# Moving half of the attention steps beside the values' product, in a fused two-block transformer kernel

## What is computed

```python
def even_mixer(h, w_in, w_out):                 # the first layer, "e" in the kernel
    qkv = (h @ w_in).reshape(B, S, 3, 16, 64).transpose(2, 0, 3, 1, 4)
    q, k, v = rope(qkv[0]), rope(qkv[1]), qkv[2]
    a = moba_attention(q[:, :8], k[:, :8], v[:, :8])     # here: plain causal softmax attention
    b = dilated_mixture(q[:, 8:], k[:, 8:], v[:, 8:])    # three windows, mixed by their sums
    return concatenate([a, b]) @ w_out

def diff_attention(q, k, v, lam):               # the second layer, "d"
    s = einsum('bhcqd,bhckd->bhcqk', q, k) * scale       # 8 heads, two maps each (c = 0, 1)
    p = softmax(where(kpos <= qpos, s, -inf))
    a = p[:, :, 0] - lam * p[:, :, 1]
    return einsum('bhqk,bhkd->bhqd', a, v)               # v has 128 columns per head
# then rms_norm per head, times a gain, and @ w_out
```

## Time and profile before

| what | value |
|---|---|
| median of three runs | 3159.81 us (3157.5 to 3160.11) |
| the profiled execution | 3160.78 us, its span 3159.0 us |
| TensorE busy | 3105.3 us, 98% of the span |
| weight loads into TensorE | 2495.2 us, 79% |
| VectorE busy | 1584.0 us, 50% |
| ScalarE busy | 1118.4 us, 35% |
| GpSimd busy | 20.4 us, 1% |
| mean granted TensorE clock | 0.994 of 2.4 GHz |
| attention "e", from the values' product on | 110.28 to 236.96 us of the span |
| attention "d", from the values' product on | 730.45 to 864.02 us |

### The profile page before, as it was taken

How to read it: one execution, slowest core, us unless ns; L and a number is a source line. 1 busy time by engine, 2 the same in 40 slices (tenths; PEclk the granted TensorE clock), 3 DMA queues, 4 the chain that set the end, 5 groups by cost and what they waited for, 6 DMA issues and landing times.

```text
span 3159.0 us, 35038 instructions
## 1 busy us (share of the span) xinstructions
PE 3105.3 (98%) x13927; PEld 2495.2 (79%) x13932; DVE 1584.0 (50%) x2346; ACT 1118.4 (35%) x1730; POOL 20.4 (1%) x29
## 2 busy tenths in 40 slices
PE   8989999999999999999999999999999999999998
PEld 6748888887588888877788878888777888878887
DVE  5575675355566752554523463334654424453324
ACT  3254443223644432334323243322334323333322
POOL 1000000000000000000000000000000000000000
PEclk9999999999999999999999999999999999999999
DMA  5302222243022223412223223333412223223321
GB/s 189 114 8 87 100 94 97 97 140 100 1 94 94 96 98 100 139 43 93 66 95 94 94 83 102 96 94 107 121 49 78 80 94 94 88 92 99 95 94 67
DMA packets 86337, 289.30 MB, mean 92 GB/s; under 512 B 11304, under 2 KB 11320, under 8 KB 85920
## 3 DMA queue, kind: packets, MB, share of 16 engines
q1 hardware_dynamic: 83584, 278.96, 27.6%
q0 software_dynamic: 1440, 6.00, 0.5%
q10 hardware_dynamic: 1152, 2.10, 0.2%
HBM read 272.33 MB, written 2.10 MB: 87 GB/s over the span
## 4 chain that ended last, share of the span: by engine, by line
PE 94%; DVE 3%; ACT 2%; issue 1%; DMA 0%; POOL 0%; ACTq 0%; DVEq 0%; POOLq 0%
PE banks L393 74%; PE banks L455 8%; PE banks L422 3%; PE banks L729 2%; PE banks L364 1%; PE banks L533 1%; PE banks L708 1%; PE banks L502 1%; PE banks L557 1%; PE banks L545 1%; PE banks L756 0%; PE banks L782 0%; ACT prob_e L875 0%; DMA x_resid<-x_fm 0%; DVE prob_e L1396 0%
## 5 line engine op out<-in xcount | busy, mean ns | idle before, releaser
L1252 DVE TENSOR_TENSOR w_lo<-w_raw,w_hi 128x1024 fp32r<-128x1024 f32 (+1 forms) x512 | 612.4, 1207 | 915.9 <-ACT w_hi L822 914.8
L822 ACT ACTIVATE w_hi<-w_raw 128x1024 fp32r<-128x1024 f32 (+1 forms) x512 | 526.8, 1041 | 843.2 <-PE banks L393 767.3
L393 PE MATMUL banks<-h_hi,w_hi 128*128 128x512 f32 x2304 | 713.8, 391 | 10.7 <-DVE h_lo L1339 10.7
L393 PE MATMUL banks<-h_lo,w_hi 128*128 128x512 f32 x2304 | 710.7, 390 | 0.0
L393 PE MATMUL banks<-h_hi,w_lo 128*128 128x512 f32 x2304 | 710.3, 390 | 0.0
L393 PEld LDWEIGHTS banks<-h_hi,w_hi 128*128 128x128 f32 x2304 | 431.9, 188 | 100.7 <-issue 12.3
L393 PEld LDWEIGHTS banks<-h_lo,w_hi 128*128 128x128 f32 x2304 | 433.5, 188 | 90.5
L393 PEld LDWEIGHTS banks<-h_hi,w_lo 128*128 128x128 f32 x2304 | 433.4, 188 | 90.1
L393 PE MATMUL banks<-hid_hi,w_hi 128*128 128x512 f32 x668 | 206.4, 390 | 0.0
L393 PE MATMUL banks<-hid_lo,w_hi 128*128 128x512 f32 x668 | 205.8, 389 | 0.0
L393 PE MATMUL banks<-hid_hi,w_lo 128*128 128x512 f32 x668 | 205.6, 389 | 0.0
(11 more groups left out here) (278 smaller groups left out, 3170.9 us busy)
## 6 DMA issues: line engine op xcount, KB each, us to landing
w_raw<-weights SPq DMA_DIRECT2D x496, 512.0 KB, 3.6
scratch<-scratch SPq DMA_DIRECT2D x128, 64.0 KB, 2.0
w_raw<-weights SPq DMA_DIRECT2D x16, 256.0 KB, 2.6
scratch<-scratch SPq DMA_DIRECT2D x32, 128.0 KB, 2.3
x_resid<-x_fm ACTq DMA_DIRECT2D x8, 256.0 KB, 10.5
decay<-tables POOLq DMA_DIRECT2D x2, 1024.0 KB, 6.1
y_fm<-x_resid SPq DMA_DIRECT2D x8, 256.0 KB, 2.1
rope<-tables POOLq DMA_DIRECT2D x2, 512.0 KB, 4.2
```

What stands on the lines that cost most here:

```text
L393: mm = e.matmul(bank[b][:, :], wt[:, k, j * P:(j + 1) * P], a[:, kt, :], start=kt == 0 and step == 0, stop=kt == k_tiles - 1 and step == 2)
L822: e.activation(m.w_hi[u % HL][:, 0:n], m.raw[u % RAW][:, 0:n], ACT.Copy).then_inc(*mark("w_hi", u))
L1252: e.tensor_tensor(m.w_lo[u % HL][:, 0:n], m.raw[u % RAW][:, 0:n], f32(m.w_hi[u % HL][:, 0:n]), ALU.subtract).then_inc(*mark("w_lo", u))
```

## The change

Both attentions take their first 24 of 48 steps (n = -1 to 4) during the values' product, as `UNDER_VALUES` says: one call in the first unit, which only starts the generator, then four, four, three, four, three, three, three. A step follows a group of six matmuls, and where a unit has four, the fourth follows the unit. `attention_steps` starts at n = -1, so the first two pairs' scores are steps of the same list. Within a step, the loop over c now stands around values and transposes. `exp` is an entry of its own, behind the transposes' copies on ScalarE.

`AttentionBanks` deals out the banks on all engines. Beside the product there are four, 4 to 7: in "e" scores and transposes take 4, 5 and 6 in turn, in "d" scores take 4 and 5, the transposes and head squares 6; the values take 7. Behind the product the banks are dealt much as before, with the scores beginning at 2 and 3. The six buffers of probabilities lie together (two of them had lain over `h_hi`), and the transposed probabilities have two buffers, where "e" had four. The value matmul of pair g waits only for the panel of v that holds it. VectorE's list changes in the same way as ScalarE's. Removed bodies that stand in the listing above are left out here.

```diff
-            prob_at = [big + kb * K for kb in (48, 53, 58, 63)] + [h, h + 5 * K]
+            prob_at = [big + kb * K for kb in (48, 53, 58, 63, 78, 83)]
             self.prob[st] = [at(f"prob{i}_{st}", [P, TRI_N], F32, a) for i, a in enumerate(prob_at)]
-            self.prob_t[st] = [at(f"probt{i}_{st}", [P, TRI_N], F32, big + (68 + 5 * i) * K) for i in range(4 if st == "e" else 2)]
+            self.prob_t[st] = [at(f"probt{i}_{st}", [P, TRI_N], F32, big + (68 + 5 * i) * K) for i in range(2)]
             self.rope[st] = at(f"rope_{st}", [P, 2 * S], F32, big + 80 * K)
...
-    def tm(self, beside):
+    def tm(self, beside, calls=None):
         for panel in range(2):
             for n in range(DT // 2):
                 self.next_unit()
+                for _ in range(calls[4 * panel + n] if calls else 0):
+                    next(beside, None)
                 if n == DT // 2 - 1:
                     yield panel
-                next(beside, None)
+                if not calls:
+                    next(beside, None)
         for _ in beside:
             pass
+UNDER_VALUES, LAST_UNDER = (1, 4, 4, 3, 4, 3, 3, 3), 4
+class AttentionBanks:
+    def __init__(self, st):
+        self.st, self.beside_product, self.pool, self.pairs, self.turns = st, True, 0, 0, 0
+    def from_pool(self):
+        self.pool += 1
+        return 4 + self.pool % 3
+    def scores(self):
+        if not self.beside_product:
+            self.pairs += 1
+            return 2 * (self.pairs % 2), 2 * (self.pairs % 2) + 1
+        return (self.from_pool(), self.from_pool()) if self.st == "e" else (4, 5)
+    def turn(self):
+        if not self.beside_product:
+            self.turns += 1
+            return 4 + self.turns % 2
+        return self.from_pool() if self.st == "e" else 6
+    def values(self, g):
+        return 7 if g <= LAST_UNDER - 2 else 6 + (g + 1) % 2
+def under_values(steps, do):
+    yield
+    for what, g, i, c in steps:
+        if what != "step_done":
+            do(what, g, i, c)
+            continue
+        yield
+        if (g, i) == (LAST_UNDER, 0):
+            return
 def attention_steps(st):
-    yield "inverse", 0, None
-    for kb in reversed(range(TB)):
-        yield "normalise", 0, kb
-    for n in range(1, DT + 3):
+    for n in range(-1, DT + 3):
         for kb in reversed(range(TB)):
             if n + 1 < DT:
...
+                yield "scores", n + 1, kb, None
+            for c in range(2 if st == "e" else 1):
+                if 2 <= n < DT + 2:
+                    yield "values", n - 2, kb, c
+                if 1 <= n <= DT:
+                    yield "transpose", n - 1, kb, c
+            if n + 1 < DT:
+                yield "exp", n + 1, kb, None
+            if 0 <= n < DT:
                 if kb == TB - 1:
-                    yield "inverse", n, None
-                yield "normalise", n, kb
+                    yield "inverse", n, None, None
+                yield "normalise", n, kb, None
             if st == "d" and n >= 3 and kb == 2:
-                yield "head_squares", n - 3, None
+                yield "head_squares", n - 3, None, None
             if kb:
-                yield "finish_some", None, None
+                yield "finish_some", None, None, None
+            yield "step_done", n, kb, None
         if st == "d" and n in HEAD_BATCHES:
-            yield "finish_next", *HEAD_BATCHES[n]
+            yield "finish_next", *HEAD_BATCHES[n], None
     if st == "d":
-        yield "finish_some", None, None
-        yield "finish_some", None, None
+        yield "finish_some", None, None, None
+        yield "finish_some", None, None, None
...
-    def gemm_tm(st, hi, lo, ready, evacuated, beside):
+    def gemm_tm(st, hi, lo, ready, evacuated, beside, calls=None):
...
+                steps = calls[4 * panel + kt0 // 2] if calls else 1
...
+                        if steps > 1 and (k, pair[0]) != (1, 2):
+                            next(beside, None)
                 if kt != DT - 1:
                     mm.then_inc(*mark("gemm", ("unit", u)))
-                next(beside, None)
+                if steps in (1, 4):
+                    next(beside, None)
         for _ in beside:
...
-        turn = {"s": 0, "t": 0}
-
-        def scores(g, i, score_banks=(0, 1, 2, 3)):
-            b = [score_banks[2 * (turn["s"] % 2) + c] for c in range(2)]
-            turn["s"] += 1
+        banks = AttentionBanks(st)
+        def scores(g, i):
+            b = banks.scores()
             width = (i + 1) * P
             w.wait_ge(*after("masks", 0))
             for c in range(2):
...
                          start=st == "e", stop=True, skip_group_check=True).then_inc(*mark("scores", (st, g, i, c)))
                 freed[b[c]] = ("exp" if st == "d" else "neg_max", (st, 2 * g + c, i))
...
+        def transpose(g, kb, c):
+            b, slot = banks.turn(), (2 * g + c) % len(prob)
             bank_is_free(b)
...
+            for i in range(kb, TB):
+                w.wait_ge(*after("normed", (st, 2 * g + c, i)))
+                t = e.transpose(bank[b][:, (i - kb) * P:(i - kb + 1) * P],
+                                prob[slot][:, TRQ[i] + kb * P:TRQ[i] + (kb + 1) * P], m.ident[:, :])
+            t.then_inc(*mark("transposed", (st, g, c, kb)))
+            freed[b] = ("probt_act" if (kb + c) % 2 == 0 else "probt_dve", (st, g, c, kb))
+        def values(g, kb, c):
+            b, width = banks.values(g), P // results
+            bank_is_free(b)
+            w.wait_ge(*after("v_act", (st, g // 4, 3)))
+            w.wait_ge(*after("v_dve", (st, g // 4, 2)))
+            w.wait_ge(*after("probt_act" if (kb + c) % 2 == 0 else "probt_dve", (st, g, c, kb)))
+            o = e.matmul(bank[b][c * width:(c + 1) * width, kb * P:S], v[:, kb, g * P + c * width:g * P + (c + 1) * width],
+                         prob_t[(g * results + c) % len(prob_t)][:, TRI[kb]:TRI[kb] + (TB - kb) * P],
+                         start=kb == TB - 1, stop=kb == 0, skip_group_check=True)
             if kb == 0:
-                freed[b] = ("o_copy", g) if st == "d" else ("o_lo", (st, g))
+                o.then_inc(*mark("values", (st, g, c)))
+                if c == results - 1:
+                    freed[b] = ("o_copy", g) if st == "d" else ("o_lo", (st, g))
...
-        gemm_tm(st + "v", m.h_hi, m.h_lo, ready, lambda panel, t: ("v_act" if t % 2 else "v_dve", (st, panel, t)), early_scores())
+        steps = attention_steps(st)
+        gemm_tm(st + "v", m.h_hi, m.h_lo, ready, lambda panel, t: ("v_act" if t % 2 else "v_dve", (st, panel, t)),
+                under_values(steps, do), UNDER_VALUES)
+        banks.beside_product = False
+        for what, g, i, c in steps:
+            do(what, g, i, c)
...
-        def scores(g, i):
+        def exp(g, i):
             width = (i + 1) * P
             for c in range(2):
-                n, b = 2 * g + c, score_banks[2 * (turn["s"] % 2) + c]
+                n = 2 * g + c
                 p = prob[n % len(prob)][:, TRQ[i]:TRQ[i] + width]
                 w.wait_ge(*after("neg_max", (st, n, i)))
                 if st == "e":
...
                                  accum_out=m.col(n, 1, i)).then_inc(*mark("exp", (st, n, i)))
                     continue
                 if g == 2:
-                    w.wait_ge(*after("gemm", ("tm", st + "v", 1, 3)))
+                    w.wait_ge(*after("roped", (st + "k", DT - 1)))
                 if g >= 3 and c == 0:
                     w.wait_ge(*after("transposed", (st, g - 3, c, 0)))
                 if g >= 3 and c == 1:
                     w.wait_ge(*after("normed", (st, 2 * (g - 3), 0)))
-                e.activation(p, bank[b][:, 0:width], ACT.Exp, bias=m.col(n, 0, i),
+                e.activation(p, bank[scored[c]][:, 0:width], ACT.Exp, bias=m.col(n, 0, i),
                              accum_out=m.col(n, 1, i)).then_inc(*mark("exp", (st, n, i)))
...
+        def transpose(g, kb, c):
+            b = banks.turn()
+            if (kb + c) % 2 == 0:
+                w.wait_ge(*after("transposed", (st, g, c, kb)))
+                width = (TB - kb) * P
+                e.activation(prob_t[(g * results + c) % len(prob_t)][:, TRI[kb]:TRI[kb] + width], bank[b][:, 0:width],
+                             ACT.Copy).then_inc(*mark("probt_act", (st, g, c, kb)))
+            b = banks.values(g)
...
+            if what == "scores":
+                scored = banks.scores()
+            elif what == "exp":
+                exp(g, i)
...
-                n, b = 2 * g, score_banks[2 * (turn["s"] % 2)]
-                turn["s"] += 1
+                n, (b, _) = 2 * g, banks.scores()
```

More of the change, by code:

```diff
@@ L924, in finish_heads, with do @@
             yield
[L926 to L933 removed]
+        finishing, scored, banks = iter(()), None, AttentionBanks(st)
+        def do(what, g, i, c):
+            nonlocal finishing, scored
+            if what == "scores":
+                scored = banks.scores()
+            elif what == "exp":
```

(18 more changed lines are left out.)

202 lines of the change are left out of this document (59 added, 143 removed).

## The result

| | us | against before |
|---|---|---|
| before, median | 3159.96 (3157.5 to 3160.47) | |
| after, median of 4 | 3196.47 (3195.66 to 3198.28) | ratio 1.0117, 95% interval 1.0104 to 1.0129 |
| after, span of the profiled execution | 3193.9 | before 3159.0 |

The change makes the kernel 36.5 us slower. The forecast was +24 us (3184). Its range, 3161 to 3200, holds the time. The sign and the two main causes were right, and 12 us were missing.

What follows compares the result with a forecast made beforehand. TensorE carries 94% of the chain and was taken to bound the kernel. Terms of +15.5 us in e and +8.4 in d summed to +23.9, giving 3184 us, with a range of 3161 to 3200.

Steps and rivals of the forecast that it cites:

- Is there anything to fill: e's stretches up to n=5: 80.7 us of TensorE work against 92.6 used, so better overlap can return 12 us there.
- Part 1, interruptions: Each entry of a step into the product costs TensorE 0.23 us: 5.5 us in e, 2.9 us in d.
- Part 2, the parted halves: e's value halves, with a transpose between, no longer run side by side: 3.38 us per head pair, seven times, 23.7 us.
- the upper bound for a lone half: In e, one value half alone costs 1.01 us at 512 columns, the price of the pair.
- Rival B: e's parted halves cost less, a lone half at d's price without form changes: 10.6 us, 3171 us; chance 0.17.
- Part 3, e's waits: e's waits for banks at the second panel's start (0.65 us) and the exit (1.1): 1.8 us together; masking is hidden.
- Part 4, d's single pair: Under d's product, scores on banks 4 and 5 wait for the previous step's exponentials: 18.6 us, bounds zero and 28.
- Clock 1.00 over both products: Expected sign in the trace: TensorE's mean clock at 1.00 over the values' products of both e and d.
- d behind the product: Exponentials behind the transposes' copies end TensorE's short waits there: -3 of 44.62 us, bounds 0 and -5.
- A: The forecast itself: e's parted halves and d's single banks cost what they show, 3184 us, range 3172 to 3198; chance 0.57.
- D: d's waits pull the clock down: ten more microseconds of matmuls at half speed, waits half longer, 3199 us; chance 0.12.
- C: The covered fill wins, with halves, transposes and banks at no price: -10 us each in e and d, 3140; chance 0.11.

Runs made afterwards that it cites:

- e6: The changed kernel with only eight score steps under the product in both attentions, e's value halves together, exponentials behind the copies: 3148.8 us, ratio 0.9964.
- e1: The changed kernel with e's two value halves of a step issued together again, then both transposes: 3174.8 us, ratio 1.0045.
- e3: The kernel before with the parting alone: e's value halves each followed by a transpose, all behind the product: 3179.0 us, ratio 1.0060.
- e2: The changed kernel with only d's first eight score steps under the product, on two pairs of banks, e unchanged: 3178.8 us, ratio 1.0059.
- e4: The changed kernel with 14 of d's steps under the product, two per unit, single score pair kept, e unchanged: 3183.2 us, ratio 1.0073.
- e5: The changed kernel with e's value halves together (24 steps), d's eight steps under the product, exponentials ahead of the copies in both: 3159.7 us, ratio 0.9997.
- e11: e6 with ScalarE's exponentials ahead of the transposes' copies in d only, still behind them in e: 3150.6 us, ratio 0.9967.
- e12: e6 with ScalarE's exponentials ahead of the transposes' copies in e only, still behind them in d: 3155.2 us, ratio 0.9982.
- e7: The changed kernel with e's 24 steps joined and started two groups later, first scores behind the product in banks 0 and 1, d eight steps: 3155.6 us.

## Why the prediction was right in sign and 12 us short

**Is there anything to fill: right.** 12 us were counted as open in e; e6 takes 10 of them. e1's period of 8.50 is the one worked out from the earlier trace rows.

**Part 1, interruptions: right.** e1: product 43.57, 8 periods of 8.50, entries 5.5, waits 8.0 make 125.1, measured 126.5. The other 1.4 us are no more than what the clock takes (0.98 over the first 92 us of e in e1, 1.8 us), so nothing speaks against the entries' 0.23. The six product matmuls of after between 170.57 and the next scores at 172.14 take 1.57 where they cost 1.36 undisturbed, 0.21 more.

**Part 2, the parted halves: right.** 3.38 us a head pair forecast, 3.31 measured (11.81 in e3 against 8.50 in e1), so 23.2 for seven where the forecast had 23.7. Between whole stretches 21.5 (e1, in after's setting) and 17.5 (e3, in before's) are left of it, since the parted order waits less: 7.6 us in after against 8.0 in e1, 4.8 in e3 against 7.9 before. The choice of the upper bound for a lone half, 1.01 us, was the one that mattered: measured 1.00 and, at 128 columns, 0.36 (e.g. 173.20 to 173.56) where the pair took 0.37. Its reason was weaker than it sounds: the earlier trace rows has no output under 128 columns and could not show that the output's width is free; after and e3 show it. Rival B, which priced a lone half at d's rate without changes of form, fell (and by its own terms it was 7 x 1.54, 10.8 us, and not 10.6). The Trainium skill, TensorEngine Tiling (Array Packing), section Tiling Modes, has the change of tiling mode drain the engine, and in Overview a gain of up to two by packing. The trace fits both: 1.01 for the pair against 1.00 for either half, and transposes at 0.59 for four against 1.02 for eight, so 0.16 us go with each change.

**Part 3, e's waits: mis-sized.** 1.8 us forecast, 6.7 measured inside the product (2.9 + 2.1 + 1.7). Behind it e took 46.35 us where the forecast had 44.0: a mean clock of 0.96 costs 1.7 to 1.9, and two waits for VectorE's copies 0.9. In the forecast's own terms two steps failed. The masking is hidden by "a value half and a transpose" only where value halves run: the three waits of 2.1 us in all lie between 140.9 and 152.8 us, in n = 1, which has none. And the list began with the steady part: the first step waits 2.9, because VectorE then still has rotary operations and a weight split before it. The exit's wait was foreseen but is for VectorE's copy of v, not for ScalarE's (1.7 against 1.1).

**Part 4, d's single pair: mechanism right, sum right by luck.** Inside the product 104.9 against a forecast of 100.4. The profile counts 14.3 us of waits (the three rows above, and 0.6 twice for VectorE's copies of v) against 18.6, and 4.4 of them are the first one's, which the forecast had at 1.45. One 512-column step in after, and behind it the product group and masks of a step that waits for nothing:

```profile
804.84 1.13 PE L583 MATMUL banks<-k_d,q_d 64*128 64x512 f32 x4
805.90 0.49 PE L603 MATMUL banks<-probt_d,v_d 128*128 128x128 f32 x2
...
806.25 0.71 PE L503 MATMUL banks<-w_hi,h_hi 128*128 128x512 f32 x2
...
808.14 0.23 PE L578 MATMUL banks<-masks_bf 128*128 128x128 bf16 x1 [0.25 <-ACT prob_d L929]
808.81 0.23 PE L578 MATMUL banks<-masks_bf 128*128 128x128 bf16 x1 [0.44 <-ACT prob_d L929]
808.97 0.92 PE L583 MATMUL banks<-k_d,q_d 64*128 64x384 f32 x4
...
848.99 0.72 PE L503 MATMUL banks<-w_hi,h_hi 128*128 128x512 f32 x2
...
850.68 0.49 PE L583 MATMUL banks<-k_d,q_d 64*128 64x128 f32 x4
```

From the scores' end at 805.90 to the next scores at 808.97 are 3.07 us, exactly the chain of the forecast. Six product matmuls and two masks take 2.72 us here and 1.69 there: 1.03 us are lost, of which the profile counts 0.69 as idle, since the modelled ends of the records before each wait cover the rest. The same comparison over all steps under d's product gives about 21 us, some 2 of them the clock's, so about 19 us of waiting against the 18.6: the first wait was 3 to 4 us longer than forecast and the others together as much shorter. This also places most of the busy time: of TensorE's 90.2 us in this stretch 81.8 were forecast, about 4.5 are waiting that counts as busy, and the lower clock over 5.6 and 4.0 us costs (0.30 x 5.6) + (0.43 x 4.0) = 3.4 us. The clock is the term that the forecast left out of its sum ("Clock 1.00 over both products"; it was 1.00 in e and 0.97 in d). That spacing and number of the steps on the single pair carry the loss is shown by e2 and e4 together: -18.3 and -12.6 us in d.

**d behind the product: size right, reason mostly wrong.** 42.35 against 44.62, -2.3 where I had -3. The 2.5 us wait of a transpose near the first square root is gone, as forecast, but a head square waits 1.5 us in its place, and all waits together went only from 5.5 to 4.5. The rest is the clock: 0.96 against 0.92 is some 1.9 us. e5 and e11 show d as short with the exponentials first. For e I had written that nobody on TensorE waits for the exponentials there. That is so, and I did not draw the consequence: moving them back brings the copies forward, which is worth 7.8 us in e with eight steps (e11 against e12). The forecast for after contains this only because it sums TensorE's work without before's 7.9 us of waits.

**The rivals.** A holds, with 12 us more. D's mechanism is there, in small: 3.4 us in d and some 1.8 in e of lower clock, over three stretches; against D the forecast had that TensorE stays two thirds busy; it was busy for 90.2 of the 104.9 us in d, and the lower clock came all the same. The time is near D's 3199 by the sum of A's misses, not by D's terms. C decided "once parting plus waits come under 20 us"; measured are 21.5 + 6.7 + 14.3 = 42.5. e5 has no parting and no single pair and lands at 3159.7, not at C's 3140: C had also assumed that waits stay at zero with 24 interruptions in e, and e1, e5 and e7 show that they don't (8 to 9 us).

What was short of the measured 36.5: 5.8 us in e (mainly the waits inside, 4.9, and clock and waits behind, 2.3, less 1.4 for a slightly lower price of parting and for transposes that cost 0.17 less where the product follows them), 5.3 in d (3.4 of them clock), and 1.5 in the choice between profiled execution and median.

## What to carry to other kernels

Two matmuls that fill half of the array each must stay neighbours in TensorE's queue: look in the trace for pairs that cost what one costs before putting anything between them. Before work is moved under a long product, look at what the other engines still have queued there, since the first step waits for that backlog and the lower clock can follow. A short cover, here eight steps, and on the in-order engine the copy that TensorE waits for ahead of the work that nobody waits for yet, together took nearly the whole gain in e; either alone took little of it. And where profiles differ by a few microseconds, take out the clock's share before looking for a cause.

## What the runs showed of the hardware

The size of a lone half surprised me only by its exactness (1.00 against 1.01 us for two). What brings the lower clock, the waits alone do not tell. After and e1 have the same wait for VectorE's backlog at e's second score step (2.87 and 2.85 us, ending at 122.33 and 122.18 us). Over 123.8 to 127.3 us, behind it, the clock is 1.00 in after and 0.51 in e1, and 10 matmul records lie there against 19. In e12 the clock falls within 165 to 170 us (0.57), behind waits of 1.09 and 0.46 us, while e11 has waits of 1.09, 0.59 and 0.84 us in the same fill and keeps 1.00; over the 5 us ahead, 160 to 165, TensorE is busy for 3.71 and 3.91. Behind the fall the busy time says nothing more (13.7 of 15 us in e12, 13.6 in e11), since the lower clock itself stretches the matmuls. The Trainium skill, Perfetto Trace Analysis, section Matmul Optimizations, asks for matmuls back to back because the engine "dynamically scales power based on utilization"; the direction agrees with the falls behind waits here, but which wait is followed by one is not in these rows.
